# Routing from rows that are not yet normalised, expert matrices requested at other points, and more products of constants

## What is computed

```python
n1 = _rmsnorm(h, norm1_g) * (1.0 + sc1) + sh1
h = h + g1 * _mixer(n1, ...)
n2 = _rmsnorm(h, norm2_g) * (1.0 + sc2) + sh2        # per token: x / rms(x), then gain and shift by column
moe = _hier_moe(n2, w_grp, b_grp, w_er, b_er, w1, w3, w2)
h = h + g2 * moe
return _rmsnorm(h, final_g)

# in _hier_moe
gp = softmax(xt @ w_grp + b_grp)                     # 8 groups, the best one is taken
el = (xt @ w_er + b_er)                              # 64 experts, the best two within that group
hdn = silu(xblk @ w1[e]) * (xblk @ w3[e])            # for the rows that were routed to expert e
out = hdn @ w2[e]
```

## Time and profile before

| What | Value |
|---|---|
| Time, median of 3 runs (lowest to highest) | 2557.52 us (2554.7 to 2561.12) |
| The profiled execution, its own time | 2557.04 us |
| Its span, first to last instruction | 2555.2 us, so 1.84 us lie around it |
| PE busy | 2328.1 us (91%) |
| DVE, ACT, POOL busy | 871.1, 743.8, 767.6 us |
| Moved by DMA | 597.28 MB |
| Mean granted TensorE clock | 0.968 of full |

### The profile page before, as it was taken

The page is one execution under the profiler, slowest core; times in us unless marked ns, Lnnn a source line. Parts: engine busy times, 40 slices in busy tenths (PEclk is TensorE's granted clock), DMA queues, the critical chain, the costliest instruction groups (busy, mean ns, idle before and its releaser), DMA issues.

```text
span 2555.2 us, 26554 instructions
## 1 busy us (share of the span) xinstructions
PE 2328.1 (91%) x10932; PEld 1432.8 (56%) x10932; DVE 871.1 (34%) x1401; ACT 743.8 (29%) x1194; POOL 767.6 (30%) x488
## 2 busy tenths in 40 slices
PE   7999889999999999999999996989888888888885
PEld 5677557788887787777777863333222222222221
DVE  2634552100014899847775233111111111111113
ACT  4434552322223423448675222100000000000101
POOL 3233543454553344334334624110000010000000
PEclk9999999999999999999999997999999999999997
DMA  5243313433323332343345257999999999999995
GB/s 176 104 175 137 107 31 132 165 116 99 105 73 115 96 100 58 122 137 116 132 136 213 101 205 254 414 427 426 425 427 425 426 426 426 425 424 424 422 426 203
DMA packets 171864, 597.28 MB, mean 234 GB/s; under 512 B 15907, under 2 KB 94755, under 8 KB 146016
## 3 DMA queue, kind: packets, MB, share of 16 engines
q1 hardware_dynamic: 154992, 562.23, 56.5%
q10 hardware_dynamic: 6080, 23.89, 2.4%
q0 software_dynamic: 10672, 9.46, 1.3%
HBM read 591.00 MB, written 28.96 MB: 243 GB/s over the span
## 4 chain that ended last, share of the span: by engine, by line
PE 54%; DMA 28%; DVE 12%; ACT 4%; issue 2%; POOL 0%; SPq 0%; ACTq 0%; DVEq 0%; POOLq 0%
DMA arena<-in_w 21%; PE ps L780 11%; PE ps L782 11%; PE ps L781 11%; PE ps L1310 7%; DVE ps L2223 4%; DMA ring<-in_w 4%; PE ps L1308 2%; PE ps L1329 2%; ACT arena L1412 1%; PE ps L862 1%; PE ps L831 1%; ACT arena L1702 1%; PE ps L852 1%; PE ps L977 1%
## 5 line engine op out<-in xcount | busy, mean ns | idle before, releaser
L2651 POOL TENSOR_TENSOR ring_r<-ring,ring_r 128x1024 fp32r<-128x1024 f32 x220 | 513.1, 2339 | 677.1 <-ACT ring_r L1401 676.9
L780 PE MATMUL ps<-r,ring_r 128*128 128x512 f32 (+1 forms) x1536 | 610.5, 397 | 2.2 <-DVE arena L2211 1.2
L782 PE MATMUL ps<-r,ring_r 128*128 128x512 f32 (+1 forms) x1536 | 599.1, 390 | 0.0
L781 PE MATMUL ps<-r,ring_r 128*128 128x512 f32 (+1 forms) x1536 | 598.7, 390 | 0.0
L1412 ACT ACTIVATE arena<-ps 128x512 f32<-128x512 f32 (+4 forms) x279 | 187.2, 692 | 1140.6 <-PE ps L1310 852.3
L1310 PE MATMUL ps<-arena 128*64 128x512 f32 x672 | 324.6, 638 | 84.8 <-DMA arena<-in_w 81.1
L1308 PE MATMUL ps<-arena 128*64 128x512 f32 x672 | 331.2, 639 | 4.1 <-issue 4.1
L780 PEld LDWEIGHTS ps<-r,ring_r 128*128 128x128 f32 (+1 forms) x1536 | 287.2, 187 | 79.4 <-issue 14.8
L781 PEld LDWEIGHTS ps<-r,ring_r 128*128 128x128 f32 (+1 forms) x1536 | 287.4, 187 | 64.1 <-issue 4.3
L782 PEld LDWEIGHTS ps<-r,ring_r 128*128 128x128 f32 (+1 forms) x1536 | 287.1, 187 | 62.9
L1401 ACT ACTIVATE ring_r<-ring 128x1024 fp32r<-128x1024 f32 x220 | 222.9, 1015 | 314.4 <-PE ps L782 215.8
(11 more groups left out here) (353 smaller groups left out, 2356.3 us busy)
## 6 DMA issues: line engine op xcount, KB each, us to landing
arena<-in_w SPq DMA_DIRECT2D x105, 2048.0 KB, 34.3
ring<-in_w SPq DMA_DIRECT2D x87, 2048.0 KB, 39.6
ring<-in_w_ada SPq DMA_DIRECT2D x12, 2048.0 KB
ring<-in_ffn_w_in SPq DMA_DIRECT2D x22, 1024.0 KB
ring<-in_w_in SPq DMA_DIRECT2D x40, 512.0 KB
ring<-in_w_in SPq DMA_DIRECT2D x8, 2048.0 KB
ring<-in_fox_w_in SPq DMA_DIRECT2D x7, 2048.0 KB
arena<-acs_d SPq DMA_DIRECT2D x16, 512.0 KB, 3.6
```

The costliest lines, as they stand in the source:

```text
L780: e.matmul(out, wh[:, k, :], X.hi[:, k0 + k, :], start=first and k == 0, stop=False)
L781: e.matmul(out, wh[:, k, :], X.lo[:, k0 + k, :], start=False, stop=False)
L782: m = e.matmul(out, wl[:, k, :], X.hi[:, k0 + k, :], start=False, stop=last and k == nk - 1)
L2651: e.tensor_tensor(GL[t], grans[t][1], GH[t].bitcast(F32), ALU.subtract).then_inc(sem["gr_lo"], 1)
```

## The change

1. **Routing.** The logits are made from `x2b` itself. The gain (`SC`) goes into the routing matrix beforehand (`RWG`), the shift times the matrix is a row that is added (`cr`, `RBC`), and 1/rms is a factor per token at the end. Logits of tile k follow two `mo` tiles behind. `tok` tiles of `x2b` alone are turned, half of them within `mo`. ACT multiplies the turned rows by 1/rms and stores them. Gain and shift are applied to the gathered rows in `XT`, with columns `SH2` and `SC2` that are read back from DRAM in another order. Several vector steps are batched or reordered.
2. **The write of `mod`** to `g2_d` now holds 24 columns (3072 single numbers) and stands behind the store of `x2` at the start of the second block.
3. **Requests.** `ring9` is in another order. Requests 2 to 4 wait for the last `so` tile (the stage before `mo`), 5 and 6 for the last `mo` tile, 7 and 8 also for the first gather. POOL starts the gathers on `TOKROW` alone.
4. **Products of constants** in `k` tile 7, before `xb`, in steps 2, 7, 32 and 33 of the attention, and before `ln`, `pos` and `list`.

```diff
@@ memory
-        EW = [A[:, 11264 + WC * i:11264 + WC * (i + 1)] for i in range(3)]
+        EW = [A[:, 12288 + WC * i:12288 + WC * (i + 1)] for i in range(3)]
...
+        ring9 = [ring9[i] for i in (0, 1, 4, 8, 6, 3, 2, 5, 7)]
@@ PE
+                    if (stage, j) == ("k", 7):
+                        fill(3, "nm", i, 0)
...
+            fill(7, "xb")
             spread("x", "xb")
...
-                    filler(PS[64:128, 7, 0:256], (2, 0, 0, 1)[m % 4])
+                    filler(PS[64:128, 7, 0:256], (2, 0, 0, 1)[m % 4] + {2: 2, 7: 3}.get(m, 0))
+                else:
+                    filler(PS[64:128, 7, 0:256], (5, 2, 0)[m - 32])
...
+            fill(4, "ln")
             sums_by_token("ln")
...
+            def logits(k):
+                w.wait_ge(sem["rwg"], 1)
+                w.wait_ge(ps("mo", k).free, ps("mo", k).n + 1)
+                for tt in range(4):
...
+                    m = e.matmul(u.ap[:, 0:72], x2b[:, k, tt * 128:(tt + 1) * 128], RWG[:, k, :], start=k == 0, stop=k == 7)
...
             for nt in range(8):
                 whole("mo", nt, X=XM)
+                if nt == 0:
+                    u = ps("cr")
+                    w.wait_ge(sem["rw"], 16)
+                    w.wait_ge(u.free, u.n)
+                    for k in range(8):
+                        m = e.matmul(u.ap[:, 0:72], modcol(3, k).broadcast_to([128, 128]), RW[:, k, :], start=k == 0, stop=k == 7)
+                    m.then_inc(u.full, 1)
+                if nt >= 2:
+                    logits(nt - 2)
+                if nt in (5, 6):
+                    for tt in (0, 1) if nt == 5 else (2, 3):
+                        by_token(tt, 0)
+            logits(6)
+            logits(7)
+            by_token(0, 1)
+            by_token(1, 1)
             sums_by_token("n2")
-            fill(2, "n2b")
-            spread("n2", "n2b")
...
+            by_token(2, 1)
+            by_token(3, 1)
+            fill(16, "pos")
             u = ps("pos")
             w.wait_ge(sem["ohs"], 1)
...
+            fill(4, "list")
             u = ps("list")
@@ ACT
             e.dma_start(a["x2_d"], x2).then_inc(sem["spill"], 16)
+            u = ps("adb", 11)
+            w.wait_ge(u.free, u.n + 1)
+            e.dma_start(a["g2_d"].rearrange("o (k p) -> p (o k)", p=128), MOD[:, 24:48], allow_slow_non_contiguous=True).then_inc(sem["g2"], 16)
...
+            w.wait_ge(sem["g2"], 16)
+            for i, dst in enumerate((SH2, SC2)):
+                e.dma_start(dst, a["g2_d"][:, D * i:D * (i + 1)].rearrange("o (p k) -> p (o k)", p=128)).then_inc(sem["g2"], 16)
...
+            by_token(0, 1)
+            by_token(1, 1)
+            root(ps("n2"), "n2", D, early=False)
+            by_token(2, 1)
+            by_token(3, 1)
...
+            for tt in range(4):
+                e.activation(n2t[tt].rearrange("t (k p) -> t p k", k=8), h2t[:, tt, :].rearrange("t (p k) -> t p k", k=8), ACT.Identity,
+                             scale=ST[:, tt:tt + 1]).then_inc(sem["nrow"], 1)
+                w.wait_ge(sem["nrow"], tt + 1)
+                e.dma_start(a["n2_d"][tt * 128:(tt + 1) * 128, :], n2t[tt]).then_inc(sem[f"n2d{tt % 2}"], 16)
...
-            e.dma_start(a["g2_d"].rearrange("o (k p) -> p (o k)", p=128), MOD[:, 40:48], allow_slow_non_contiguous=True).then_inc(sem["g2"], 16)
@@ DVE
+                if nt == 1:
+                    u2 = ps("cr")
+                    w.wait_ge(u2.full, u2.n + 1)
+                    e.tensor_tensor(RBC, u2.ap[:, 0:72], P("rb"), ALU.add).then_inc(u2.free, 1)
...
+                e.scalar_tensor_tensor(LG[:, tt, :], u.ap[:, 0:72], ST[:, tt:tt + 1], RBC, ALU.mult, ALU.add).then_inc(u.free, 1)
...
-                    e.tensor_copy(XT[i][:, 4 * half:4 * half + 4, :], cols(u.ap, 4)).then_inc(u.free, 1)
+                    for j in range(4):
+                        k = 4 * half + j
+                        m = e.tensor_scalar(XT[i][:, k, :], u.ap[:, 128 * j:128 * j + 128], SC2[:, k:k + 1], SH2[:, k:k + 1], ALU.mult, ALU.add)
+                    m.then_inc(u.free, 1)
@@ POOL
-            w.wait_ge(sem["list"], 3)
+            w.wait_ge(sem["list"], 2)
@@ SP
                 elif i < 9:
-                    u = ps("mo", 7)
+                    u = ps("so" if i < 5 else "mo", 7)
                     w.wait_ge(u.full, u.n + 1)
-                    if i == 8:
...
-                        u = ps("mx", 1, 1)
-                        w.wait_ge(u.free, u.n + 1)
+                    if i == 4:
+                        w.wait_ge(sem["m_hi"], 8)
+                    if i == 7:
+                        w.wait_ge(sem["xg0"], 16)
```

More of the change, by code:

```diff
@@ L301, in bank_table @@
         t("so", nt, skip={ps("rx").bank})
[L302 to L307, removed]
-    for tt in range(4):
[L309 to L315, removed]
+    t("mo", 0)
+    t("cr")
+    t("mo", 1)
+    for tt in range(4):
+        t("lg", tt)
+    held = {ps("lg", tt).bank for tt in range(4)}
+    for nt in range(2, 8):
+        t("mo", nt, skip=held)
+        if nt in (5, 6):
+            for tt in (0, 1) if nt == 5 else (2, 3):
+                t("tok", tt, 0, skip=held)
+    t("tok", 0, 1, skip=held)
+    t("tok", 1, 1, skip=held)
+    t("n2", skip=held)
+    t("tok", 2, 1, skip=held)
+    t("tok", 3, 1, skip=held)
+    t("pos")
     t("list")
@@ L1249, in pe @@
[L1249 to L1261, removed]
@@ L1807, in act, with by_token @@
                     e.activation(mH[:, nt, :], ymix2[:, nt, :], ACT.Copy).then_inc(sem["m_hi"], 1)
+            def by_token(tt, half):
+                evict(h2t[:, tt, 512 * half:512 * half + 512], ps("tok", tt, half), ACT.Copy)
             for nt in range(8):
@@ L1819, in act @@
-            u = ps("lg")
-            evict(LGT, u, ACT.Copy, src=u.ap[0:72])
-            def by_token(tt, what):
-                for half in range(2):
-                    u = ps("tok", tt, half, what)
-                    if what == "n2":
-                        dst = n2t[tt % 2].rearrange("t (k p) -> t p k", k=8)[:, 64 * half:64 * half + 64, :]
-                        evict(dst, u, ACT.Copy, src=u.ap.rearrange("t (p k) -> t p k", k=8))
-                    else:
-                        evict(h2t[:, tt, 512 * half:512 * half + 512], u, ACT.Copy)
@@ L2438, in dve @@
[L2438 to L2445 removed]
+            bc = lambda x, n: x.broadcast_to([128, 4, n])
+            u = ps("n2")
@@ new lines, in dve @@
+            w.wait_ge(u.free, u.n + 1)
+            e.reciprocal(ST[:, 0:4], ST[:, 0:4]).then_inc(sem["nr"], 1)
+            e.memset(PRE[:, 0, :], 0.0).then_inc(d.next(), 1)
+            w.wait_ge(sem["nr"], 1)
+            w.wait_ge(ps("cr").free, ps("cr").n + 1)
+            for tt in range(4):
+                u = ps("lg", tt)
+                w.wait_ge(u.full, u.n + 1)
+                e.scalar_tensor_tensor(LG[:, tt, :], u.ap[:, 0:72], ST[:, tt:tt + 1], RBC, ALU.mult, ALU.add).then_inc(u.free, 1)
@@ L2504, in dve @@
                 e.tensor_tensor(ASN[i], OH[i], bc(val, 64), ALU.mult).then_inc(sem["asn"], 1)
+            u = ps("pos")
+            w.wait_ge(u.full, u.n + 1)
+            for i in range(2):
+                e.tensor_tensor(OHS if i else msel, OH[i], cols(u.ap[:, 0:256], 4), ALU.mult).then_inc(d.next(), 1)
+            for i, seat in enumerate((tmp1, tmp2)):
+                two_back()
+                e.tensor_reduce(seat, OHS if i else msel, AX, ALU.add).then_inc(d.next(), 1)
+            for i, seat in enumerate((tmp1, tmp2)):
+                two_back() if i == 0 else last()
+                e.tensor_tensor(SEAT[:, i], i64, bc(seat, 64), ALU.is_equal).then_inc(sem["seat"], 1)
+            e.tensor_copy(CNT, u.ap[:, 256:320]).then_inc(u.free, 1)
             u = ps("list")
@@ L2754, in pool @@
                 for half in range(2):
-                    for what in ("n2", "h2"):
-                        u = ps("tok", tt, half, what)
-                        w.wait_ge(u.full, u.n + 1)
+                    u = ps("tok", tt, half)
+                    w.wait_ge(u.full, u.n + 1)
             rows(0)
```

169 lines of the change are left out of this document (70 added, 99 removed).

## The result

| | before | after |
|---|---|---|
| median (range, runs), us | 2560.94 (2554.7 to 2568.0, 8) | 2547.03 (2544.9 to 2552.5, 8) |
| profiled execution, us | 2557.04 | 2546.90 |
| its span, us, and mean granted clock | 2555.2, 0.968 | 2545.1, 0.966 |

The ratio is 0.9945, with a 95% interval of 0.9933 to 0.9958: the changed kernel is 13.9 us faster. Forecast were 23.5 us, and 2547.0 lies just outside the range of 2526 to 2546. The passage between the two stages moved as forecast; a part of its gain was given back right behind it.

What follows compares the result with a forecast made beforehand. PE was taken to bound the kernel before the passage, DMA the experts after it. DMA full 25.2 us sooner, less 4.9 and 1.5, plus 4.7 from products of constants: 23.5 off 2557.0, so 2533.5 us, range 2526 to 2546.

Steps and rivals of the forecast that it cites:

- Products of constants: Added PE products in waits before `xb`, in the attention and before `ln` hold the clock: 4.7 us gained, bounds 0 to 6.
- Work within `mo`: Routing work added to PE while it is full makes the last `mo` tile end 10.9 us later (9.5 to 14).
- Routing after it: From the last `mo` tile's end to `TOKROW` takes 21.2 us, so `TOKROW` is ready at 1543.5 instead of 1554.9.
- The wait for `pos`: DVE's wait in the routing after `mo` falls from 6.45 to 1.4 us.
- Stores level with the list: The fourth store of rows, issued at 1538.5, takes 5 us and lands at 1543.5, when `TOKROW` is ready.
- Rival 1: Stores end the chain: the fourth lands 11 us after issue, the gather starts 6 us later, 2539.5 us; chance 0.14.
- `TOKROW` to request 9: From `TOKROW` at 1543.5, through gather and the first expert's products, to request 9 at 1560.8.
- The moved write: The 3072 small numbers sent at about 826, behind the store of `x2`, cost nothing; bounds 0 and 36 us.
- rivals 2 and 3: Small writes reach PE in part, 2543.5 us, chance 0.08; or they stop PE, 2569.5 us, chance 0.04.
- The hush of 36 us: By count, the moved small writes let little else through the DMA engines for 36 us, to about 868.
- the sum ends at request 9: Requests 9 and 10 wait for the first expert, leaving the DMA engines a hole of 1.5 us; full engines otherwise.
- rival 4: Matrices are held by slots, that is by PE, so the earlier start is not passed on: 2552.3 us; chance 0.04.

Runs made afterwards that it cites:

- b_fills: The kernel before with nothing but the added products of constants; ratio 0.9985 to the kernel before, 3.9 us less.
- a_latereq: The changed kernel with requests 2 to 4 again made behind the last `mo` tile; 2563.7 us, ratio 0.9984 to the kernel before.
- a_nofills: The changed kernel without the added products of constants at `xb`, `k` tile 7, attention and `ln`; ratio 0.9990 to the kernel before.

## Why the prediction came out as it did

*Products of constants: 4.7 forecast, 6.0 found between the means of 5 and 12 profiles.* Right as a sum, not in its parts. Of the earlier trace rows only the attention's place behaved as said in this profile (clock 1.00 from 373 to 380). The fill before `xb` itself ran at the lower clock, 6.23 us for what I took as 3.3 in a wait of 3.81, with 0.53 from 16 to 23; behind `ln` 0.66 from 1074 to 1079 (1.00 in b_fills). I had computed a gain from a clock that one execution happened to have: in this pair of profiles it showed as 1.2.

*Work within `mo`: 10.9 forecast, 13.6 here, 10.4 where the clock stayed.* The wait for the routing matrix was 2.1 as forecast, and its price was mis-sized: I charged the wait and not the clock behind it, which fell in seven of ten profiles, though the earlier trace rows show just that behind waits of 2.5 us. `cr` took 3.69 instead of 2.0. The last copy of `mo` came at 1523.8 (1511.4 in the earlier trace rows).

*Routing after it: 21.2 forecast.* DVE finished `TOKROW` at 1543.9, 20.1 behind the last copy. The wait for `pos`, 6.45 in the earlier trace rows and forecast at 1.4, was 0.72.

*Stores level with the list.* Right: the fourth was issued at 1540.4 and the gather went at 1544.2. Rival 1 did not happen, for the reason given against it. But that reason was an effect of the change, the early requests, which I had priced by matrices alone; a_latereq shows 12.6 us there.

*`TOKROW` to request 9: 17.3 forecast (1543.5 to 1560.8), 18.2 found (1543.9 to 1562.1).*

*The moved write: nothing.* Right. In this window PE is busy for 12.00 of 12.00 at clock 1.00; the 3072 numbers were through by 837, no further weight part was requested before 846.6, and rivals 2 and 3 are gone:

```profile
831.00:837.00 6.00, 6.00 (x24) 4.04 (x24) 5.76 (x9) 2.92 (x5) 0.00 (x0) 0.90 0.62 136
837.00:849.00 12.00, 12.00 (x53) 9.33 (x52) 6.56 (x14) 7.76 (x9) 4.81 (x3) 1.00 0.07 2
```

The hush of 36 us did not come; scaling the 12 us by count was wrong, and so was putting all 12 down to the writes. That such writes slow a load beside them the runs bear out (8.5 us from request to landing without them, 13.2 to 15.0 with them); by what mechanism they do it, no run here shows.

*The step that failed: the sum ends at request 9.* For the hole behind it I took 1.5 us and went straight on at full engines. Requests 11 and 12 hang on the second expert, which I never priced; the earlier trace rows ended at the first expert's copy, and the next row of that view in before, shown above, has the second 15.7 us later, with "remote" as what ended the wait. Before, it was covered by a late ninth matrix. The change took the cover away, and 6 us of the gain with it in this profile: a hole of 6 us where the sum has 1.5, ahead of requests 11 and 12 and not ahead of 9 and 10. Beside a control, taking the hold-up away gave 7.4 and 8.0 us. This is rival 4, the gain not passed on because matrices are held by PE, come true in part: I gave it 0.04 because of the share of 1.01 in the earlier trace rows, which is a fact about 1640 to 2496 and says nothing of the first twelve matrices.

The sum for this pair of profiles: 23.5, less 3.5 for the products of constants, 2.7 for `mo` and 6 for the hold-up, plus 1.1 for the routing, is 12.4; 10.1 were found, and some 2 stay unassigned. On chip 1, without hold-up, the changed kernel gained 22.9. That this is near to 23.5 is in part luck: the mean gain of the products is above its term, and in that profile `mo` took 10.4, nearly what I had said, because the clock happened to stay up.

What stays open is how the scatters delay PE's signals, and why they did not in the session on chip 1. In a_nofills (copies 27.2) PE started 6 products in 6 us while the DMA engines did nothing, so it is not their bandwidth:

```profile
1584.00:1590.00 6.00, 4.16 (x6) 0.78 (x5) 0.00 (x0) 0.00 (x0) 4.48 (x6) 0.50 0.02 0
```

A late load of instructions is not seen either: the next one on that queue comes 4.2 us behind ACT's third copy in the changed kernel and in a_again alike. That PE slows down only after several of its signals are pending fits all these profiles, but no run tests it. Whether an execution without the profiler is held up at the same place no trace can show; the times say so only through the medians.

## What to carry to other kernels

When an edit makes a stage start sooner, follow the chain of requests until it is in steady state, and read for each request which wait ends last; a stall that was free may stand right behind the one you remove. Put bookkeeping transfers that nobody waits for where much is queued ahead, spread out, not at the head of a pipeline. And price a wait on PE with the clock behind it, and a clock effect from several executions, not from one.

## What the runs showed of the hardware

- 24 indirect DMAs of 128 single numbers in a row from POOL, one every 1.29 us, went with four signals of PE that came 9 to 21 us late and with PE's issue at one product in 1 to 2 us, in every such profile at the head of the loop on chips 9 and 14 and in the first pair. In the three on chip 1 they did not. 12 in a row: four signals 3.4 to 4.7 us late and PE's pace untouched. One per turn: nothing.
- A wait of PE of 2.0 to 2.2 us behind full work was followed by 6.8 us at clock 0.50 in seven of ten profiles; without the wait the clock stayed at 1.00 there in three of three.
- A store of 512 KB took 4.6 us from issue to landing with the DMA engines otherwise nearly empty, 15.7 beside loads of 2 MB.
- The same program had a ratio of 0.9905 in one session on chip 1, and 0.9940 and 0.9941 in sessions on chips 9 and 14, with intervals that don't touch in the first and the last. Whether it is the chip or the session is not shown.
